# Moving two of the four weight sums of each Strassen job from VectorE to accumulating DMAs

## The reference, cut to what matters

```python
def swiglu_half(x, pre_g, w_gate, w_up, w_down, post_g):
    h = rms_norm(x, pre_g)
    u = jax.nn.silu(h @ w_gate) * (h @ w_up)
    return x + 0.5 * rms_norm(u @ w_down, post_g)
```

## Time and profile before

| | |
|---|---|
| time, median of 3 runs | 1250.32 us (1250.29 to 1253.73) |
| the profiled execution's own time | 1250.35 us |
| its span, first to last instruction | 1248.6 us |
| TensorE busy | 1188.5 us, 95% of the span |
| VectorE busy | 929.9 us, 74% |
| ScalarE busy | 639.2 us, 51% |
| GpSimd busy | 99.7 us, 8% |
| mean granted TensorE clock | 0.982 |
| mean DMA rate | 84 GB/s |

### The profile page before, as it was taken

The page is one execution under the profiler, slowest core; times in us unless marked ns, Lnnn a source line. Parts: engine busy times, 40 slices in busy tenths (PEclk is TensorE's granted clock), DMA queues, the critical chain, the costliest instruction groups (busy, mean ns, idle before and its releaser), DMA issues.

```text
span 1248.6 us, 22101 instructions
## 1 busy us (share of the span) xinstructions
PE 1188.5 (95%) x8460; PEld 1126.8 (90%) x8460; DVE 929.9 (74%) x1394; ACT 639.2 (51%) x1250; POOL 99.7 (8%) x128
## 2 busy tenths in 40 slices
PE   6999999999989999999998999999999999999877
PEld 6999999999989799999965679989999999999876
DVE  7988999899888734644357551279889998998856
ACT  5565655565555423132266443345666555655544
POOL 2000000000000003604034001110000000000000
PEclk8999999999999899999999999999999999999989
DMA  8224224313323312423200001232242243133222
GB/s 254 69 68 136 68 84 121 102 56 115 102 76 131 90 51 68 92 55 91 76 14 24 24 1 35 68 110 68 69 135 69 85 119 102 59 112 102 77 102 76
DMA packets 162549, 104.72 MB, mean 84 GB/s; under 512 B 16907, under 2 KB 160352, under 8 KB 161936
## 3 DMA queue, kind: packets, MB, share of 16 engines
q1 hardware_dynamic: 161344, 101.50, 28.2%
q0 software_dynamic: 1088, 1.84, 0.5%
q10 hardware_dynamic: 16, 0.00, 0.0%
HBM read 95.06 MB, written 8.27 MB: 83 GB/s over the span
## 4 chain that ended last, share of the span: by engine, by line
PE 78%; DVE 11%; issue 4%; ACT 4%; DMA 2%; SPq 0%; DVEq 0%; POOL 0%; ACTq 0%
PE PS L641 43%; PE PS L391 17%; PE PS L683 4%; ACT WQ_HI L740 3%; PE PS L409 2%; PE PS L2250 2%; PE PS L2221 2%; DVE SB L787 2%; PE PS L2236 1%; DMA RAWP<-in_ff_w_up 1%; DVE TU L866 1%; DVE SB L791 1%; DVE UF L1068 1%; PE PS L1944 1%; PE PS L1596 1%
## 5 line engine op out<-in xcount | busy, mean ns | idle before, releaser
L641 PE MATMUL PS<-HHI,WQ_HI 128*128 128x288 f32 x1120 | 332.8, 297 | 8.0 <-ACT SNQ L722 3.9
L641 PE MATMUL PS<-HLO,WQ_HI 128*128 128x288 f32 x1120 | 331.1, 296 | 0.0
L641 PE MATMUL PS<-HHI,WQ_LO 128*128 128x288 f32 x1120 | 330.0, 295 | 0.0
L641 PEld LDWEIGHTS PS<-HHI,WQ_HI 128*128 128x128 f32 x1120 | 210.2, 188 | 10.9 <-ACT WQ_HI L740 6.6
L740 ACT ACTIVATE WQ_HI<-SB 128x512 fp32r<-128x512 f32 (+2 forms) x288 | 163.9, 571 | 105.2 <-PE PS L641 60.2
L641 PEld LDWEIGHTS PS<-HHI,WQ_LO 128*128 128x128 f32 x1120 | 211.2, 189 | 0.0
L641 PEld LDWEIGHTS PS<-HLO,WQ_HI 128*128 128x128 f32 x1120 | 210.4, 188 | 0.0
L641 PE MATMUL PS<-UHI,WQ_HI 128*128 128x288 f32 x616 | 187.2, 304 | 11.8 <-DVE ULO L853 9.3
L641 PE MATMUL PS<-ULO,WQ_HI 128*128 128x288 f32 x616 | 184.3, 299 | 0.0
L641 PE MATMUL PS<-UHI,WQ_LO 128*128 128x288 f32 x616 | 184.3, 299 | 0.0
L740 ACT ACTIVATE WQ_HI<-RAWP 128x512 fp32r<-128x512 f32 (+2 forms) x216 | 121.7, 564 | 41.0 <-PE PS L641 34.2
(11 more groups left out here) (384 smaller groups left out, 2164.9 us busy)
## 6 DMA issues: line engine op xcount, KB each, us to landing
RAWP<-in_ff_w_gate SPq DMA_DIRECT2D x44, 512.0 KB, 4.0
RAWP<-in_ff_w_up SPq DMA_DIRECT2D x44, 512.0 KB, 5.3
RAWP<-in_ff_w_down SPq DMA_DIRECT2D x24, 768.0 KB, 4.4
RAW<-in_w_in SPq DMA_DIRECT2D x21, 512.0 KB, 3.8
x_spill<-X SPq DMA_DIRECT2D x2, 2304.0 KB, 9.2
XOLD<-x_spill SPq DMA_DIRECT2D x2, 2304.0 KB, 9.7
RAWP<-in_ff_w_down SPq DMA_DIRECT2D x8, 512.0 KB, 3.4
RAW<-in_w_out SPq DMA_DIRECT2D x8, 512.0 KB, 4.0
```

Of the source, the lines that this page charges most:

```text
L641: last = nc.tensor.matmul(PS[:, bank, 0:HT], w, h, start=i in (P1, P7, P2) and k == 0 and s == 0, stop=k == n - 1 and s == 2, skip_group_c ...
```

## The change

`weight_sums` keeps only its first instruction. SyncE now also loads the two quarters A11 and A12 of each job from HBM into slots 2 and 3 of `SB` (`sum_loads`), and GpSimd issues two DMAs from `SB` to `SB` that add what they carry to what is there (`sums_pool`): first slot 1 onto slot 2, then, after the first has landed, slot 2 onto slot 3. The high splits are ordered P7, P2, P5, P4, P6 and P3; the low splits are grouped P7 with P5 and P6 with P3. `low_early_sums` stands behind the evacuation `ev22`. `XOLD` is loaded ahead of the weights of the last job instead of behind them. In the second half-step six pieces of `XOLD` are turned inside the last jobs and four behind them. Some instructions at the edges of the half-steps change places.

```diff
+SPLIT_RANK = {P7: 1, P2: 2, P5: 3, P4: 4, P6: 5}
 def nth_low(r, i):
     n = 2 * NPLAIN + 4 * since(r)
-    if i in (P7, P6):
+    if i in (P7, P5):
         return n + 2
     if i in (P2, P4):
         return n + 3
     return n + (4 if r in SOLO or r + 1 == NJ else 5)
...
+                if r:
+                    sum_loads(sp, f, r - 1, srcs)
+                if kind == "g":
+                    srcs = [gv[:, 4 * i:4 * i + 4, x * P:(x + 1) * P] for i in range(2)]
+                else:
+                    srcs = [dv[:, 2 * lo + i:2 * hi:2, 2 * q * P:(2 * q + 1) * P] for i in range(2)]
...
-            sp.wait_ge(*f["used"].at(nth_product(GJOB[JF - 1], P3)))
-            sp.wait_ge(*f["moved"].at(16))
-            sp.dma_start(XOLD[:].rearrange("p k t -> p (k t)"), spill).then_inc(f["moved"].sem, 16)
+                if r == NJ - 2:
+                    sp.wait_ge(*f["used"].at(nth_product(GJOB[JF - 1], P3)))
+                    sp.wait_ge(*f["moved"].at(16))
+                    sp.dma_start(XOLD[:].rearrange("p k t -> p (k t)"), spill).then_inc(f["moved"].sem, 16)
+            sum_loads(sp, f, NJ - 1, srcs)
...
         def weight_sums(dve, f, r):
...
+                dve.wait_ge(*f["s_added"].at(32 * since(r)))
             quarter, at_ = quarters(r)
             nc.vector.tensor_tensor(wides(SB[:, 0:2], n), quarter[:, 0:4:3],
                                     quarter[:, at_[A21]:at_[A21] + 1].to_broadcast([P, 2, n, P]),
                                     ALU.add).then_inc(f["s_done"].sem, 1)
-            dve.wait_ge(*f["s_done"].at(3 * since(r) + 1))
-            nc.vector.tensor_tensor(wide(SB[:, 2], n), wide(SB[:, 1], n), quarter[:, at_[A11]],
-                                    ALU.add).then_inc(f["s_done"].sem, 1)
-            dve.wait_ge(*f["s_done"].at(3 * since(r) + 2))
-            nc.vector.tensor_tensor(wide(SB[:, 3], n), wide(SB[:, 2], n), quarter[:, at_[A12]],
-                                    ALU.add).then_inc(f["s_done"].sem, 1)
+
+        def sum_loads(sp, f, r, srcs):
+
+            if r < NPLAIN:
+                return
+            if r == NPLAIN:
+                sp.wait_ge(*f["w_lo"].at(2 * NPLAIN))
+            else:
+                sp.wait_ge(*f["w_lo"].at(nth_low(r - 1, P3)))
+                sp.wait_ge(*f["s_added"].at(32 * since(r)))
+            for i, src in enumerate(srcs):
+                sp.dma_start(wide(SB[:, 2 + i], width(r)), src).then_inc(f["sb_in"].sem, 16)
+
+        def sums_pool(pool, f):
+            for r in range(NPLAIN, NJ):
+                n = width(r)
+                pool.wait_ge(*f["sb_in"].at(32 * (since(r) + 1)))
+                pool.wait_ge(*f["s_done"].at(since(r) + 1))
+                pool.dma_start(wide(SB[:, 2], n), wide(SB[:, 1], n), accum_op=ALU.add).then_inc(f["s_added"].sem, 16)
+                pool.wait_ge(*f["s_added"].at(32 * since(r) + 16))
+                pool.dma_start(wide(SB[:, 3], n), wide(SB[:, 2], n), accum_op=ALU.add).then_inc(f["s_added"].sem, 16)
+                pool.wait_ge(*f["s_added"].at(32 * since(r) + 32))
...
-        OLD_PIECES = {0: {P2: 0, P5: 1, P4: 2, P1: 3}, 1: {P2: 4, P5: 5, P4: 6, P1: 7}, 2: {P2: 8, P5: 9}}
+        OLD_PIECES = {0: {P4: 0, P1: 1}, 1: {P2: 2, P4: 3}, 2: {P2: 4, P4: 5}}
...
         def fpost_pe(pe, p):
             if p is fpost[0]:
-                keep_busy(7, 8)
-                cache_pe(pe)
-                keep_busy(1, 2)
+                keep_busy(1, 6)
             if p is fpost[1]:
-                for t, k0, k1 in ((0, 0, 6), (2, 0, 6), (1, 0, 6)):
-                    new_turned(pe, t, k0, k1)
+                old_turned(pe, 6)
+                new_turned(pe, 0, 0, 6)
+                old_turned(pe, 7)
+                new_turned(pe, 2, 0, 6)
+                new_turned(pe, 1, 0, 6)
+                old_turned(pe, 8)
```

More of the change, by code:

```diff
@@ L733, in weight_hi @@
             if i in S_OF:
-                act.wait_ge(*f["s_done"].at(3 * since(r) + {P7: 1, P5: 1, P6: 2, P3: 3}[i]))
+                if i in (P7, P5):
+                    act.wait_ge(*f["s_done"].at(since(r) + 1))
+                else:
+                    act.wait_ge(*f["s_added"].at(32 * since(r) + (16 if i == P6 else 32)))
                 src = wide(SB[:, S_OF[i]], n)
@@ L978, in ffn_act @@
                         y_scaled(act, p, 2 * q - 1)
-                old = OLD_PIECES.get(r - URGENT - 1, {}) if f is ff[1] and r + 1 < NJ else {}
+                old = OLD_PIECES.get(r - URGENT - 1, {}) if f is ff[1] else {}
                 weight_hi(act, f, r + 1, P5)
-                if old:
+                if P2 in old:
                     old_copied(act, old[P2])
                 weight_hi(act, f, r + 1, P4)
-                if old:
-                    old_copied(act, old[P5])
+                weight_hi(act, f, r + 1, P6)
                 if r + 1 not in SOLO:
                     snap(act, f, r + 1, 0)
-                    if old:
+                    weight_hi(act, f, r + 2, P1)
+                    if P4 in old:
                         old_copied(act, old[P4])
-                    weight_hi(act, f, r + 2, P1)
-                    if old:
+                    if P1 in old:
                         old_copied(act, old[P1])
@@ L995, in fpost_act @@
             if p is fpost[1]:
-                old_copied(act, 2 * TT - 2)
-                old_copied(act, 2 * TT - 1)
+                for n in (6, 7):
+                    old_copied(act, n)
             y_square(act, f, p, KD // 2 - 1, 1)
@@ L1002, in fpost_act @@
                 y_scaled(act, p, KD - 2)
+                old_copied(act, 8)
             if p is fpost[0]:
                 split_hi_first(act)
+            post_act(act, p)
+            if p is fpost[0]:
                 cache_act(act)
-            post_act(act, p)
+            if p is fpost[1]:
+                old_copied(act, 9)
         def h_factors(dve, f, e, gain):
@@ L1157, in fpost_dve @@
             square_sum(dve, e, KD - 1)
-            dve.wait_ge(*e["root"].at(1))
-            nc.vector.reciprocal(INV[:], ROOT[:]).then_inc(e["inv"].sem, 1)
             if p is not None:
@@ L1162, in fpost_dve @@
                 split_lo(dve, MIX0 + 1)
-                cache_dve(dve)
+            dve.wait_ge(*e["root"].at(1))
+            nc.vector.reciprocal(INV[:], ROOT[:]).then_inc(e["inv"].sem, 1)
             dve.wait_ge(*f["moved"].at(32))
@@ L1352, in old_turned @@
             c, rows = FRAMES[t]
-            bank = OLD_BANKS[n % 2]
+            bank = OLD_BANKS[n]
             if n == 0:
                 pe.wait_ge(*ff[1]["moved"].at(32))
-            if n >= 2:
-                pe.wait_ge(o["old_copied"], n - 1)
+            if n == 6:
+                pe.wait_ge(*ff[1]["ev11"].at(NJ - NPLAIN))
+                pe.wait_ge(*ff[1]["snap"].at(3 * (NJ - NPLAIN)))
+            elif n >= 2:
+                pe.wait_ge(o["old_copied"], n - 1 if n < 6 else n)
             for k in range(4):
@@ L1366, in old_copied @@
             act.wait_ge(o["old_T"], n + 1)
-            nc.scalar.activation(XTOK[0:rows, t, 4 * P * h:4 * P * (h + 1)], PS[0:rows, OLD_BANKS[n % 2], :],
+            nc.scalar.activation(XTOK[0:rows, t, 4 * P * h:4 * P * (h + 1)], PS[0:rows, OLD_BANKS[n], :],
                                  ACT.Copy).then_inc(o["old_copied"], 1)
@@ L1397, in finish_pe @@
                 new_turned(pe, t, 6, KD)
+            old_turned(pe, 9)
             for t in range(3, TT):
@@ L2383, in out_act @@
                     split_hi(act, B_OUT + m + 2)
+                elif m + 2 == KD:
+                    plain_high(act, ff[1], 0, 0)
+                    plain_high(act, ff[1], 0, 1)
         def out_dve(dve):
@@ L2403, in _ @@
             start_pool(pool)
+            sums_pool(pool, ff[0])
             cache_pool(pool)
@@ L2408, in _ @@
             post_pool(pool, post)
+            sums_pool(pool, ff[1])
         @block.scalar
@@ L2439, in _ @@
             plain_low(dve, ff[1], 0, 0)
+            plain_low(dve, ff[1], 0, 1)
+            plain_low(dve, ff[1], 1, 0)
             post_dve(dve, post)
```

38 lines of the change are left out of this document (18 added, 20 removed).

## The result

The changed kernel takes 1531.38 us (median of 4 runs, 1528.83 to 1538.94), the kernel before 1251.78 in the same comparison (4 runs): 1.2243 times as long, 95% interval 1.2194 to 1.2291. The prediction was 1375, slower, in a range of 1295 to 1485. The direction and the mechanism came out; the size was 156 us short, and the time lies 46 us above the range.

A forecast was written before the change was run, and what follows sets the result against it. A once-a-job ring of loads, two transfers and splits was taken to bound the kernel. From 1250.35, +147 (ring, queue) -9.2 -9.8 -1.6 +1 +2.3 -4.0 -0.6 gave 1375 us; range 1295 to 1485.

The forecast's parts named there:

- The ring: Once a job: loads, two transfers, ScalarE's P3 split, VectorE's P6-P3 split; 12.15 us at width 4 against TensorE's 11.2.
- The transfer term: Each accumulating SBUF transfer in the ring: 3.0 us for 256 KB, 2.8 at width 3, 2.5 at width 2.
- the rival of 3.8 us: Long transfers in the ring: 3.8 us each, from second operand, weight traffic or GpSimd's descriptors; 1484 us, chance 0.12.
- The time of 1538: Case of long transfers: each waits for one VectorE instruction of 1.22 us, so takes 4.2 us.
- The hand-overs: Between members of the ring: six at 0.05 us, 0.3 us a job.
- The queue term: Quarter loads queue behind weights on SyncE: 1 to 1.6 us late in some nine jobs, 10 us a half-step.
- The floor: P6 waits 0.5 us for its late low split in each of 68 jobs: 35 us, inside the ring's excess.
- The gains: Time given back: VectorE waits 9.2 us, XOLD 9.8, pieces 1.6, half-step beginnings 4.0 and 0.6; tail costs 2.3.
- The first edge: Behind the first half-step, fewer fillers before the frame sums bring the first post-norm instruction 4.0 us earlier.
- the term of 0.6: Gain from the similar edit ahead of the second half-step: 0.6 us.
- The step into the last chunk: Ring step before the last chunk of down jobs: hidden in the 4.7 us wait there, so put at nothing.
- The lower clock: Idle gaps of 2 to 4 us might lower TensorE's granted clock, likeliest in width 2 jobs; would make the prediction wrong.

The follow-up runs named there:

- the old pairs: Changed kernel with both transfers, but low splits paired as before (P7 with P6, P5 with P3): 1541.16 us, ratio 1.2288.
- the small weights: Changed kernel with weight loads from the seventh job on cut to an eighth (gate, up) or one piece (down): 1465.10 us, ratio 1.1738.
- the kernel with the edges: Changed kernel with all four weight sums on VectorE, old pairs and high-split order, early pair in its old place: 1239.38 us, ratio 0.9913.
- the last experiment: Fastest kernel (1229.22 us: VectorE sums, old pairs, edges, early split behind `ev22`) with the old order behind the first half-step: 1230.73 us, ratio 0.9843.

## Why the prediction was wrong

**The ring was right.** Four kernels that shorten it by different members (loads, traffic, overlap, addition) shorten the sum of the rounds by 154, 61, 58 and 63 us and the time by 163, 66, 60 and 76. The kernel whose edit does not shorten it, the old pairs, gained nothing.

**The transfer term was mis-sized.** "I take 3.0 us" for 256 KB, 2.8 and 2.5 for the smaller ones: undisturbed they take 3.28, 2.98 and 2.66, and in the mean of the rounds 3.65 us. A transfer of 1 us more was priced at 136 us, so this is 105 us. Undisturbed transfers would have been 32 us too long (two in each of 38, 22 and 8 rounds, by 0.28, 0.18 and 0.16 us); the other 73 are disturbance, of which the small weights took 48 away. Another 12 fall on two transfers. The prediction charged 1 us for XOLD's traffic "beside the accumulates of job 35"; in both half-steps the first of these was under way with it, and took 8.2 and 10.0 us for 192 KB. The second one (timelines of SyncE and GpSimd):

```profile
1462.78 0.44 SPq L601 DMA_DIRECT2D XOLD<-x_spill  x1
```

```profile
1465.82 0.86 POOL L821 DMA_DIRECT2D SB<-SB  x1 [15.79 <-DMA SB<-in_ff_w_down]
1476.09 0.86 POOL L823 DMA_DIRECT2D SB<-SB  x1 [9.40 <-DMA SB<-SB]
```

Some 13 us of disturbance remain without a cause shown.

The row that I leaned on, a load of 256 KB from outside at 3.0 us, turned out near for the wrong reason: a plain copy inside the chip takes 2.3, and the second operand adds the 1.0 that makes it 3.3. The second operand and the weights' traffic were both named, for the rival of 3.8 us, and that rival's mechanism is what happened, at 3.65. VectorE, the third point named for it, showed nothing.

The time of 1538, from transfers of 4.2 us, is nearest to the result by coincidence. Its mechanism, that a transfer waits for a VectorE instruction, did not show: the second accumulate of the round behind the one above was issued at 335.76 and landed at 339.07, the 3.3 us of any undisturbed one, while VectorE was busy almost without a break (these two timelines, GpSimd and VectorE):

```profile
335.76 0.86 POOL L823 DMA_DIRECT2D SB<-SB  x1 [2.70 <-DMA SB<-SB]
```

```profile
335.96 1.23 DVE L780 TENSOR_TENSOR WQ_LO<-SB,WQ_HI 128x1024 fp32r<-128x1024 f32 x1 [0.53 <-ACT WQ_HI L752]
337.10 0.45 DVE L1168 TENSOR_TENSOR UF<-SNS,PS 128x288 f32<-128x288 f32 x1
337.47 1.35 DVE L888 TENSOR_TENSOR ULO<-TU,UHI 128x1152 fp32r<-128x1152 f32 x1
338.74 1.22 DVE L771 TENSOR_TENSOR WQ_LO<-RAWP,WQ_HI 128x1024 fp32r<-128x1024 f32 x1
```

The estimate from the Trainium skill, page "DMA: Bandwidth & Descriptors", section "Anatomy of one DMA — SWDGE (gpsimd) path", of 2.6 us lies between the two that were measured, 2.3 for a copy and 3.3 for an accumulate, and the measurement decides. The rule that the prediction took from the Trainium skill, page "SBUF — State Buffer", is for VectorE's two-port modes, and its section "Who interferes with whom" says that `tensor_tensor` has none. All four instructions above are `tensor_tensor`; they fit that, and they are no test of the rule.

**The hand-overs were mis-sized.** "Six hand-overs at 0.05 us" are right between engines (0.03 to 0.08 us here) and wrong for GpSimd: 0.52 us from the landing of the loads to its issue, 0.28 us from one transfer to the next. The two make 48 of the 56 us by which the hand-overs are longer in the rounds, and that was in neither bound: the range varied the transfer alone.

**The queue term was about right**, 20 us allowed and 12 found, since the loads of quarters do wait behind weights (up to 6.3 us), though the weights' harm to the accumulates, which travel at the same time, was left to a rival.

**The floor** of 35 us is 58 by itself, and does lie inside the ring: the old pairs, which remove it, gained nothing.

**The gains.** XOLD's wait is gone; with the pieces, the second half-step's products are 10.9 us shorter in the kernel with the edges (11.4 predicted). Waits of VectorE 9.2, measured 10.2. Tail 2.3, measured 1.9 (from P3's end to the frame sums 4.7 us, against 2.8 in the earlier trace rows). The first edge is shown by the timeline of the changed kernel, where the last product ended its issue at 553.44:

```profile
553.57 4.04 PE L439 MATMUL PS<-FILL 128*128 128x384 f32 x12
557.44 1.50 PE L412 MATMUL PS<-FILL,ACC 128*128 128x96 f32 x10
```

```profile
561.30 0.81 DVE L1198 SCALAR_TENSOR_TENSOR X<-X,GCOLS,PS 128x576 f32<-128x576 f32 x1 [1.69 <-PE PS L426]
```

It is 7.7 us from the fillers' start to the post-norm, 12.0 in the earlier trace rows: 4.3 gained, 4.0 predicted, and the working was right. But it bought nothing, as the last experiment says, and the term of 0.6 was not there either. So that the kernel with the edges came out 13.1 us faster for an expected 13.7 is partly luck: its profiled execution, at 1243.11 us, is only 7.2 us faster than that of before, and its runs spread from 1238.89 to 1243.26. The step into the last chunk was wrong as said above. All in all the error is the ring's, less what was counted twice, and 23 us outside the rounds.

**The lower clock** did not decide. The granted clock was at half for 269 us of the trace (46 before), among them the stretch behind the gap of 6.2 us before 327.93, and that is TensorE's greater busy time; but while the ring sets the pitch a slower TensorE only fills its idle time. The one place in a round where it could show is ScalarE's start of P3's split, which waits for a product too: 0.21 us behind the landing at width 4 instead of 0.08, at most 9 us in 68 rounds. This is argued from the traces; no run held the clock. What the lower clock costs outside the rounds is part of the 23 us there.
